# Adding the expert rows to the residual in DRAM with an accumulating scatter, in a retention, sparse-attention and mixture-of-experts layer

## The reference, cut to what matters

```python
def moe(h, router_w, router_b, w_gu, b_gu, w_down, b_down):
    top_vals, top_idx = lax.top_k(logits, TOP_K)
    gates = jax.nn.softmax(top_vals, axis=-1)
    ...
    def expert_block(args):
        gu = xb @ w_gu[e] + b_gu[e]
        gate, up = jnp.split(gu, 2, axis=-1)
        gate = jnp.minimum(gate, SWIGLU_LIMIT)            # 7.0
        up = jnp.clip(up, -SWIGLU_LIMIT, SWIGLU_LIMIT)
        glu = gate * jax.nn.sigmoid(SWIGLU_ALPHA * gate)  # 1.702
        return ((up + 1.0) * glu) @ w_down[e] + b_down[e]
    ys = lax.map(expert_block, ...) * rows_g[:, None]
    return jax.ops.segment_sum(ys, rows_tok, num_segments=N)

x = x + g2[:, None, :] * moe(h2)      # end of the layer
return rms_norm(x, final_g)
```

## Time and profile before

| what | us |
|---|---|
| median of 3 runs (1624.64 to 1625.86) | 1625.63 |
| the profiled execution's own time | 1622.43 |
| its span in the profile | 1620.7 |
| way to the first expert's first matmul (L1350) | 399.4 |
| last matmul of the last expert, end | 1575.9 |
| from there to the end of the span | 44.8 |

### The profile page before, as it was taken

One profiled execution on the slowest core, in us unless ns is written; L12 is line 12 of the kernel. 1 busy time (PEld: TensorE's weight loads), 2 busy tenths in 40 slices (PEclk: granted clock), 3 DMA queues, 4 the chain that ended last, 5 costly groups with the idle time before them and its releaser, 6 DMA issues.

```text
span 1620.7 us, 20692 instructions
## 1 busy us (share of the span) xinstructions
PE 1510.6 (93%) x6920; PEld 1195.8 (74%) x6920; DVE 1378.9 (85%) x1218; ACT 1115.3 (69%) x1157; POOL 340.7 (21%) x269
## 2 busy tenths in 40 slices
PE   3999987995899999999999999999999999999975
PEld 3667963454688888888888888888888888888852
DVE  4689957266699999999999999999999999999955
ACT  3544336243688878888788788887878888888741
POOL 1213510101022222223222222232222222322210
PEclk8999998995899999999999999999999999999998
DMA  9745410224599999899999998899999998999926
GB/s 344 230 143 182 181 54 12 73 103 159 195 350 372 366 367 363 346 357 362 367 368 368 377 368 350 352 367 359 371 363 371 366 360 346 361 361 375 365 90 259
DMA packets 97855, 478.96 MB, mean 296 GB/s; under 512 B 24408, under 2 KB 33728, under 8 KB 45504
## 3 DMA queue, kind: packets, MB, share of 16 engines
q1 hardware_dynamic: 86848, 456.76, 72.9%
q0 software_dynamic: 10976, 21.81, 3.8%
HBM read 475.37 MB, written 20.98 MB: 306 GB/s over the span
## 4 chain that ended last, share of the span: by engine, by line
PE 82%; DVE 10%; ACT 3%; DMA 2%; issue 1%; SPq 0%; DVEq 0%; POOLq 0%; POOL 0%; ACTq 0%
PE bank L1358 15%; PE bank L1357 14%; PE bank L1359 14%; PE bank L1379 7%; PE bank L1381 7%; PE bank L1380 7%; PE bank L1241 3%; PE bank L1339 2%; PE bank L1350 2%; PE bank L1331 2%; DVE w_lo L1480 2%; DMA ring<-in_ada_w 1%; PE bank L1062 1%; PE bank L1063 1%; PE bank L1064 1%
## 5 line engine op out<-in xcount | busy, mean ns | idle before, releaser
L1519 DVE TENSOR_TENSOR e_lo<-ring,e_hi 128x2048 fp32r<-128x2048 f32 x384 | 868.1, 2288 | 73.7 <-ACT e_hi L726 69.9
L726 ACT ACTIVATE e_hi<-ring 128x2048 fp32r<-128x2048 f32 x384 | 728.3, 1914 | 186.7 <-PE bank L1359 186.4
L1357 PE MATMUL bank<-e_hi,x_hi 128*128 128x512 f32 x1024 | 406.4, 397 | 1.5 <-DVE e_lo L1519 1.5
L1358 PE MATMUL bank<-e_lo,x_hi 128*128 128x512 f32 x1024 | 403.0, 394 | 0.0
L1359 PE MATMUL bank<-e_hi,x_lo 128*128 128x512 f32 x1024 | 399.3, 390 | 0.0
L1357 PEld LDWEIGHTS bank<-e_hi,x_hi 128*128 128x128 f32 x1024 | 192.9, 188 | 48.5 <-DVE e_lo L1519 2.4
L1358 PEld LDWEIGHTS bank<-e_lo,x_hi 128*128 128x128 f32 x1024 | 193.4, 189 | 40.2
L1359 PEld LDWEIGHTS bank<-e_hi,x_lo 128*128 128x128 f32 x1024 | 193.2, 189 | 40.4
L1379 PE MATMUL bank<-e_hi,act_hi 128*128 128x512 f32 x512 | 208.7, 408 | 4.9 <-DVE act_lo L1532 4.9
L1381 PE MATMUL bank<-e_hi,act_lo 128*128 128x512 f32 x512 | 202.2, 395 | 0.0
L1380 PE MATMUL bank<-e_lo,act_hi 128*128 128x512 f32 x512 | 201.5, 393 | 0.0
(11 more groups left out here) (249 smaller groups left out, 1788.8 us busy)
## 6 DMA issues: line engine op xcount, KB each, us to landing
ring<-in_w_gu SPq DMA_DIRECT2D x256, 1024.0 KB, 6.8
ring<-in_w_down SPq DMA_DIRECT2D x128, 1024.0 KB, 7.6
ring<-in_ada_w SPq DMA_DIRECT2D x24, 1024.0 KB, 7.3
ring<-in_w_in SPq DMA_DIRECT2D x9, 1024.0 KB, 5.9
ring<-expert_rows SPq DMA_DIRECT2D x6, 1024.0 KB, 10.8
ring<-in_w_o SPq DMA_DIRECT2D x4, 1024.0 KB, 6.6
ring<-in_w_in SPq DMA_DIRECT2D x10, 256.0 KB, 6.0
xs<-in_x SPq DMA_DIRECT2D x4, 512.0 KB, 5.1
```

The lines of the kernel that those rows point to most:

```text
L726: return nc.scalar.activation(dst, src, ACT.Copy, scale=scale)
L1357: pe.matmul(bank[b][:], x_hi[:, c, :], hi, start=False, stop=False)
L1358: pe.matmul(bank[b][:], x_hi[:, c, :], lo, start=False, stop=False)
L1519: tt(e_lo[c % PARTS][:], raw(period.raw_slot(c)), e_hi[:, c % PARTS, :].bitcast(F32), ALU.subtract).then_inc(lo_ready, 1)
```

## The change

The gates and g2 are applied when the rows leave PSUM: DVE, and no longer ACT, writes `ys` as rows times gate times g2. The gate of each of the 128 places comes from `gate_rows` in DRAM by a small indirect gather of POOL. The scatter then adds the rows in DRAM onto `sum_rows`, where the residual was stored before the loop (4 stores of 512 KB, and one of 512 KB to rows 512 to 639, which take the places without a token). SP waits for the last scatter and reads 4 tiles of 512 KB into `xs`; PE has no more work there, and only the norm follows.

The nonlinearity is rewritten as well. ACT reads the gate half straight from PSUM (`glu`: x times sigmoid of 1.702 x) and no longer waits for DVE; DVE clips the up half between -6 and 8, where the bias already holds the + 1, and forms act with one instruction, the minimum with the value at the limit and the product. The first clip and one product of DVE go, and so do ACT's copy of the rows. `gate_up` now waits for `up_ready` and `glu_ready`.

The core of the diff (declarations and renamed semaphores are left out; removed PE lines 1430 to 1439 and DVE lines 1812 to 1835 are those of the end described above):

```diff
@@ -29,6 +29,7 @@
 LIMIT, ALPHA = 7.0, 1.702
+GLU_TOP = LIMIT / (1.0 + math.exp(-ALPHA * LIMIT))
 CAP = P
@@ -103,7 +104,8 @@
     g_dram = nc.dram_tensor("g_rows", (2, D), F32, kind="Internal").ap()
-    y_dram = nc.dram_tensor("expert_rows", (S * K, D), F32, kind="Internal").ap()
+    sum_dram = nc.dram_tensor("sum_rows", (S + P, D), F32, kind="Internal").ap()
+    gate_dram = nc.dram_tensor("gate_rows", (S * K, 1), F32, kind="Internal").ap()
 
@@ -258,6 +258,9 @@
         hot32 = routes[:, 1024:1152].rearrange("p (t e) -> p t e", e=E)
+        add_i = future[:, 0:48].bitcast(I32)
+        spare_row, gate = future[:, 64:65], future[:, 65:66]
+        aidx = future[:, 66:67].bitcast(U32)
         tabT = routes[:, 1280:1408]
@@ -533,10 +534,8 @@
             sp.wait_ge(all_scattered, 1)
-            for n in range(2 * T):
-                t, cols = n // 2, half_cols(n)
-                sp.dma_start(rows_of(t)[:, :, cols], y_dram[t * P * K:(t + 1) * P * K, cols]
-                             .rearrange("(p k) d -> p k d", k=K)).then_inc(y_in[n], 16)
+            for t in range(T):
+                sp.dma_start(xs[:, t, :], sum_dram[t * P:(t + 1) * P, :]).then_inc(y_in[t], 16)
             for n in range(2 * T):
@@ -605,6 +604,9 @@
                                              base=off, pattern=[[1, 96]], channel_multiplier=-1))
+            done(nc.gpsimd.iota(spare_row, pattern=[[0, 1]], base=S, channel_multiplier=1,
+                                allow_small_or_imprecise_dtypes=True))
+            done(nc.gpsimd.memset(gate, 0.0))
             nc.gpsimd.memset(flag[0:32, :], 0.0).then_inc(late_consts, 1)
@@ -629,10 +631,14 @@
                 pool.dma_start(xn2_dram[t * P:(t + 1) * P, :], xn2[:, t, :]).then_inc(xn2_stored, 16)
+                pool.wait_ge(x2_ready, 2 * t + 2)
+                pool.dma_start(sum_dram[t * P:(t + 1) * P, :], xs[:, t, :]).then_inc(sum_stored, 16)
+            pool.dma_start(sum_dram[S:S + P, :], xs[:, 0, :]).then_inc(sum_stored, 16)
             pool.wait_ge(xn2_stored, 16 * T)
...
             last_token, last_row = pool.to_reg(S - 1), pool.to_reg(S * K - 1)
+            last_sum = pool.to_reg(S + P - 1)
 
@@ -670,16 +676,22 @@
                 choose_bias(sel_d, now, sel_d_ready)
+                pool.tensor_copy(sidx[:].bitcast(I32), dst_i[:, before]).then_inc(sidx_ready, 1)
+                pool.wait_ge(sidx_ready, 1)
+                pool.indirect_dma_start(out=gate, out_offset=None, in_=gate_dram,
+                                        in_offset=bass.IndirectOffsetOnAxis(ap=sidx[:, 0:1], axis=0),
+                                        bounds_check=last_row, oob_is_err=False).then_inc(gate_in, 16)
+                pool.sem_clear(sidx_ready)
                 pool.wait_ge(y_ready, i + 1)
...
                     pool.wait_ge(scattered, (i - 1) * 16)
-                pool.tensor_copy(sidx[:].bitcast(I32), dst_i[:, before]).then_inc(sidx_ready, 1)
-                pool.wait_ge(sidx_ready, 1)
-                pool.indirect_dma_start(out=y_dram,
-                                        out_offset=bass.IndirectOffsetOnAxis(ap=sidx[:, 0:1], axis=0),
-                                        in_=ys, in_offset=None,
-                                        bounds_check=last_row, oob_is_err=False).then_inc(scattered, 16)
-                pool.sem_clear(sidx_ready)
+                pool.tensor_copy(aidx.bitcast(I32), add_i[:, before]).then_inc(aidx_ready, 1)
+                pool.wait_ge(aidx_ready, 1)
+                pool.indirect_dma_start(out=sum_dram,
+                                        out_offset=bass.IndirectOffsetOnAxis(ap=aidx[:, 0:1], axis=0),
+                                        in_=ys, in_offset=None, bounds_check=last_sum, oob_is_err=True,
+                                        compute_op=ALU.add).then_inc(scattered, 16)
+                pool.sem_clear(aidx_ready)
 
@@ -699,6 +711,10 @@
             opening(0)
+            pool.wait_ge(gates_ready, 1)
+            pool.dma_start(gate_dram.rearrange("(t p k) o -> p t (k o)", t=T, k=K), gates[:]).then_inc(gates_stored, 16)
+            pool.wait_ge(gates_stored, 16)
+            pool.wait_ge(sum_stored, 16 * (T + 1))
             steady(1)
@@ -954,12 +970,9 @@
 
-            def sigmoid(i):
-                a.wait_ge(gate_ready, i + 1)
-                nc.scalar.activation(sg, gc, ACT.Sigmoid, scale=ALPHA).then_inc(sig_ready, 1)
-
-            def rows_out():
-                copy(ys, banks[:, 2048:3072]).then_inc(y_ready, 1)
+            def glu(i, full):
+                a.wait_ge(chunk_used, full)
+                nc.scalar.activation(sg, banks[:, 0:1024], ACT.Gelu_apprx_sigmoid).then_inc(glu_ready, 1)
 
@@ -977,21 +990,13 @@
                     hi(period, c)
-                sigmoid(i)
+                glu(i, period.at(GU))
                 x_parts(i + 1)
-                for c in range(3):
+                for c in range(PARTS):
                     hi(after, c)
-                a.wait_ge(chunk_used, i * CHUNKS + 8)
-                if i is not 1:
-                    a.wait_ge(scattered, (i - 1) * 16)
-                rows_out()
-                hi(after, 3)
 
...
                 act_parts(i)
-                a.wait_ge(chunk_used, i * CHUNKS)
-                a.wait_ge(scattered, (i - 1) * 16)
-                rows_out()
 
@@ -1017,8 +1021,9 @@
 
+            nc.scalar.activation(nmax[:, 0, 0:1], epsc[:], ACT.Sqrt)
             for t in range(T):
-                a.wait_ge(x3_ready, 2 * t + 2)
+                a.wait_ge(y_in[t], 16)
                 done(nc.scalar.activation(rows_of(t)[:, 1, :], xs[:, t, :], ACT.Square, accum_out=ss[:, t:t + 1]))
@@ -1345,7 +1350,8 @@
                 if i is not 0:
-                    pe.wait_ge(banks_free, i)
+                    pe.wait_ge(up_ready, i)
+                    pe.wait_ge(glu_ready, i)
                 for b in range(4):
@@ -1688,6 +1682,7 @@
                 v.wait_ge(bias_in, 16 * 6)
+                done(ts(b_raw[0:96, 1024:2048], b_raw[0:96, 1024:2048], 1.0, None, ALU.add))
                 done(nc.vector.tensor_copy(b_part, b_raw[0:96, :]))
@@ -1727,7 +1722,8 @@
                 done(nc.vector.tensor_copy(dst_i[:, r], dstf[:, r]))
-                return ts(tok_i[:, r], dst_i[:, r], 2, None, ALU.arith_shift_right)
+                done(ts(tok_i[:, r], dst_i[:, r], 2, None, ALU.arith_shift_right))
+                return ts(add_i[:, r], tok_i[:, r], spare_row, None, ALU.min)
             done(nc.vector.tensor_copy(dstf[:, 0:E], tabT[:, 0:E]))
@@ -1755,21 +1751,29 @@
-            done(tt(gates[:], gates[:], ri[:, 0:T].unsqueeze(2).broadcast_to((P, T, K)), ALU.mult))
+            tt(gates[:], gates[:], ri[:, 0:T].unsqueeze(2).broadcast_to((P, T, K)), ALU.mult).then_inc(gates_ready, 1)
+            v.wait_ge(last_rows_in, 32)
 
...
-                ts(gc, banks[:, 0:1024], LIMIT, None, ALU.min).then_inc(gate_ready, 1)
-                ts(uc, banks[:, 1024:2048], LIMIT, -LIMIT, ALU.min, ALU.max).then_inc(banks_free, 1)
+                ts(uc, banks[:, 1024:2048], LIMIT + 1.0, 1.0 - LIMIT, ALU.min, ALU.max).then_inc(up_ready, 1)
 
...
-                v.wait_ge(banks_free, i + 1)
-                stt(out=uc, in0=uc, scalar=1.0, in1=gc, op0=ALU.add, op1=ALU.mult).then_inc(prod_ready, 1)
-                v.wait_ge(prod_ready, i + 1)
-                v.wait_ge(sig_ready, i + 1)
-                tt(act, uc, sg, ALU.mult).then_inc(act_ready, 1)
+
+                v.wait_ge(up_ready, i + 1)
+                v.wait_ge(glu_ready, i + 1)
+                stt(out=act, in0=sg, scalar=GLU_TOP, in1=uc, op0=ALU.min, op1=ALU.mult).then_inc(act_ready, 1)
+
+            def rows_out(i, full):
+
+                v.wait_ge(chunk_used, full)
+                v.wait_ge(gate_in, i * 16)
+                if i is not 1:
+                    v.wait_ge(scattered, (i - 1) * 16)
+                stt(out=ys, in0=banks[:, 2048:3072], scalar=gate, in1=g2_row, op0=ALU.mult,
+                    op1=ALU.mult).then_inc(y_ready, 1)
 
@@ -1794,11 +1798,17 @@
                     lo(after, c)
+                rows_out(i, i * CHUNKS + 8)
+
+            def closing(i):
+                act_rest(i)
+                rows_out(i, i * CHUNKS)
 
             opening(0)
-            with v.Fori(1, E) as i:
+            steady(1)
+            with v.Fori(2, E) as i:
                 steady(i)
-            act_rest(E)
+            closing(E)
             n_over = v.value_load(over_i[0:1, 16:17], min_val=0, max_val=OVER)
```

More of the change, by code:

```diff
@@ L1004, in _ @@
             opening(0)
-            steady(1)
-            with a.Fori(2, E) as i:
+            with a.Fori(1, E) as i:
                 steady(i)
@@ L1808, in _ @@
                     steady(i)
-                act_rest(ITEMS)
-            for t in range(T):
-                for k in range(K - 1):
-                    last = ts(diag[:, t * (K - 1) + k, :], ident[:], gates[:, t, k:k + 1], None, ALU.mult)
-            last.then_inc(diag_ready, 1)
```

(16 more changed lines are left out.)

25 lines of the change are left out of this document (5 added, 20 removed).

## The result

| | before | after |
|---|---|---|
| median of the runs, us | 1625.74 (4 runs, 1624.64 to 1627.04) | 1603.39 (4 runs, 1601.52 to 1606.30) |
| ratio to before | | 0.9872, 95% interval 0.9857 to 0.9887 |
| profiled execution: span, own time | 1620.7, 1622.43 | 1603.2, 1605.01 |

The change takes 22.4 us off the medians; 23.2 were forecast. A second set of the changed kernel gave 1601.04 against 1623.43 of before beside it (0.9862, 0.9847 to 0.9877).

The account below looks back on a forecast made before the run. PE was taken as the bound in the steady periods, but not in the end; -25.1 + 1.6 + 0.2 + 0.5 - 1.2 + 0.8 + 0 = -23.2 took 1625.6 to 1602.4 us. Range 1598 to 1634, the forecast's own 1598 to 1608.

Parts of the forecast that it names:

- Step 1: From the first load to the end: 38.9 us give way to four loads and the norm in 13.8 us, -25.1.
- Step 2: The last scatter's landing of 3.25 us, now writing and reading 128 full rows: +1.6 us, bounds 0 to +5.
- 3 from the last matmul's rows to the scatter's issue: In the end, DVE takes the rows out of PSUM in place of ACT's copy: +0.2 us (0 to +1).
- Step 4: Last hand-over: rows_out ahead of act_lo costs 1.2 us, ACT's dropped wait for the clip saves 0.75: +0.5 us.
- Step 7: The 31 steady periods stay at 36.1 us: PE is the bound and the new waits have cover, worth 0.
- 5 first hand-over: After the first expert's gate_up, the sigmoid starts at once, as the clip did: -1.2 us (0 to -2.3).
- Step 6: Ahead of the loop: adding 1 to the bias on DVE 0.6 us, an extra list step 0.2: +0.8 us.
- X: Time of all 16 DMA engines that the accumulating scatter takes each period: 2.6 us, deciding the time from 3.1 on.
- rival A: Every period: the accumulate makes DMA the bound, (X - 3.1) times 31; +40 us at 4.4, +84 at 5.8; chance 0.25.
- Rivals B: Every period: the gate's gather lands late for low part 4, 31 us per us beyond about 15; chance 0.05.
- C: The end saves less: reading rows just written +4 us, accumulate landing in 8 us +3, giving 1609; chance 0.06.
- D: The activation needs a table load each period, 1.3 us more for ACT, costing nothing; no chance given.

## Why the prediction was right

Term by term, in the profiled execution of before and the two of the changed kernel:

| step | forecast | first profile | second |
|---|---|---|---|
| 1 the end, from the first load on | -25.1 | 14.4 - 38.9 = -24.5 | -24.6 |
| 2 landing of the last scatter | +1.6 | 6.38 - 3.25 = +3.1 | +2.9 |
| 3 from the last matmul's rows to the scatter's issue | +0.2 | 1.95 - 1.54 = +0.4 | +0.4 |
| 4 last hand-over, and 7 the periods, from the third expert on | +0.5, 0 | 1089.6 - 1089.3 = +0.3 | +0.3 |
| 5 first hand-over | -1.2 | 9.3 - 10.6 = -1.3 | -1.3 |
| 6 ahead of the loop, 296.6 to 384.5 before | +0.8 | 88.9 - 87.9 = +1.0 | +0.8 |
| in no term: first expert's product | | 24.6 - 24.8 = -0.2 | +1.2 |
| in no term: from the second expert's first matmul to the third | | 37.0 - 38.1 = -1.1 | -0.3 |
| in no term: last down product | | 12.9 - 13.6 = -0.7 | -0.3 |
| in no term: from the landing to the first load | | 1.5 - 1.2 = +0.3 | +0.3 |
| in no term: the front, ahead of the change | | +5.2 | +0.8 |

These make the spans' -17.5 and, within 0.1, -19.7. The seven steps come to -21.0 and -21.5, where -23.2 was forecast; over the medians of several runs it is -22.4, and the interval of the ratio reaches from -18.4 to -23.2. So the forecast of the steps was about 2 us too good, mostly by step 2, and that it came within a microsecond of the medians is in part luck: the stretches in no term, in which PE's clock differs from one execution to the next, bring -1.7 in the first profile and +0.9 in the second. The first profiled pair alone would have told a wrong size by 5 us.

*Step 1* held within its bounds. The last tile lands about 8.4 us after the first issue (8.1 for the loads of x), and 6.0 us stand behind it. The Trainium skill ("DMA: Bandwidth & Descriptors", "Anatomy of one DMA") would have had 6.8 for the landing, estimated by it; the trace shows 8.4. The section's figures are for DMAs that GpSimd issues, and these are SP's.

*Step 2* is the term that was mis-sized: 3.1 and not 1.6. I priced a second pass of the bytes at the rate of a plain store, 1.3 us. POOL's queue in the last landing of the changed kernel (6.5 us from the issue), then of the plain scatter (3.4 us):

```profile
q0 software_dynamic: 144, 0.52, 55.4%
```

```profile
q0 software_dynamic: 144, 0.52, 38.1%
```

The same 128 rows keep the 16 engines busy for 3.6 us and for 1.3, so the addition takes 2.3 us of them and not 1.3; the other 0.7 of the 3.0 pass before or behind the packets. With 57 rows the landing is the same. In a period nothing waits for it.

*Step 4* had the right mechanism. The run of the nonlinearity alone shows both sides of it: -0.9 from the shorter work, +1.2 from rows_out ahead of act_lo; I had -0.75 and +1.2.

*Step 6* came out right, though it is not a cost of the operation (0.67 us) as I had it. It lengthens a pause of PE from 0.64 to 1.35 us. The loss of clock behind the pause was there before (8.83 us for the 16 matmuls, 8.79 after), so the longer pause cost its 0.7 alone.

*Step 7* was right in its result and in X (2.6 forecast, 2.5 by the share, 2.7 by the period at the limit; with no weights beside it an accumulate takes 3.6), and wrong in its break point. (POOL came to 10.6 us of 36 and not 14, which decides nothing.) I took the busy share, 93% of 36.1 us, for the time that the transfers need. The runs with more accumulates put the need of the changed kernel at an estimated 33.2 us, though its share reads 0.98. The point is therefore X = 2.7 + 2.9 = 5.6 us and not 3.1, and a loss would have begun 0.7 us above that. So the room was wider than I thought, and of rival A, to which I gave 0.25 on that wrong limit, only the end at 5.8 was left, and there for 6 us and not 84.
The Trainium skill ("Collectives: The Full Stack", "The bandwidth ceiling: the fold count and why AG ≠ RS ≠ AR") has a reduce of the DMA engines cost 1.93 of a copy, measured there in a collective. By the shares here (gathers 9.8 - 6.9 = 2.9%, so plain scatter 5.5 - 2.9 = 2.6%, accumulate 6.9%) it is 2.65 times the plain scatter, and in the last landing 3.6 / 1.3 = 2.8: this case shows more. At the limit, counting read and written bytes alike fits: 16.0 MB in 38.7 us and 18.1 MB in 44.1 are 414 and 410 GB/s.

Rivals B, C and D did not come: the gate's gather lands in 5.6 us, rows just written are read as fast as others, and no period has a table load.

## What to carry to other kernels

A DMA share near 1 does not say that the DMA is the limit: add the suspected traffic once more, and see whether the period moves. An accumulating scatter cost the engines 2.6 to 2.8 times what a plain one did and landed 2 to 3 us later; put it where nothing waits for it. A short pause of PE ahead of long matmul work can cost more than itself through the clock: here 1.5 to 1.8 us more, as much behind 0.64 us as behind 1.36, so take it away whole. Compare stretches of the trace rather than spans when fronts differ by 5 us by chance, and take a second profile of the same kernel: what differs between the two is no effect of the change.

## What the hardware showed that was not expected

- With no weights beside it, an accumulate of 128 rows of 4 KB lands 6.0 to 6.4 us after its issue, one of 100 rows after 6.2 and one of 57 after 6.3; a plain store of 128 rows lands after 3.4 to 4.4.
- The DMA shares of two queues add up to 1.02 with PE never waiting. With two and four more accumulates the periods of 38.7 and 44.1 us are 414 and 410 GB/s, an accumulate's bytes counted twice.
- After a pause of 1.36 us 16 matmuls took 8.53 us and not 7.03, after one of 0.64 us 8.83.
- PE's clock in 210 to 270 us was 0.80 to 0.89 in executions of the same instructions; the first expert started up to 4.4 us apart in two executions of one kernel, and the spans were 2.2 us apart.
